# An encoder layer's last attention pair: the merge of three attention results spread over one unit more

## The reference, cut to what matters

```python
for w, d in ((128, 1), (512, 4), (2048, 16)):      # B heads: dilated windows
    o, lse = banded_attention(strided(q), strided(k), strided(v), ...)
w = jax.nn.softmax(jnp.stack(lses, 0), axis=0)
ob = jnp.einsum('cblh,cblhd->blhd', w, jnp.stack(outs, 0))
oa = rms_norm(oa, norm_a); ob = rms_norm(ob, norm_b)   # oa: windowed heads with a sink logit
x = layer_norm(ALPHA * x + concat([oa, ob]) @ w_out)
x = layer_norm(ALPHA * x + moe(x))                     # 16 experts, top 2, and a shared one
```

## Time and profile before

| | |
|---|---|
| median of 3 runs | 1217.55 us (1215.06 to 1222.8) |
| the profiled execution | 1218.93 us, of which 1217.1 us lie between its first and last instruction |
| PE busy | 1198.4 us (98% of the span) |
| DVE, ACT, POOL busy | 724.5, 591.5, 218.2 us |
| mean granted TensorE clock | 0.997 |
| granted TensorE clock from 590 to 620 us | 1.00 |
| PE's waits from 588 to 660 us | 2.9 us for exponentials (0.56, 0.72, 0.51, 0.49, 0.19 and 0.46), 1.2 us for the first low part of the transposes, 0.7 us for POOL's casts, 0.6 us for a residual, 0.5 us for the last results |

### The profile page before, as it was taken

The page is one execution under the profiler, slowest core; times in us unless marked ns, Lnnn a source line. Parts: engine busy times, 40 slices in busy tenths (PEclk is TensorE's granted clock), DMA queues, the critical chain, the costliest instruction groups (busy, mean ns, idle before and its releaser), DMA issues.

```text
span 1217.1 us, 22117 instructions
## 1 busy us (share of the span) xinstructions
PE 1198.4 (98%) x8040; PEld 1076.1 (88%) x8040; DVE 724.5 (60%) x1796; ACT 591.5 (49%) x1463; POOL 218.2 (18%) x276
## 2 busy tenths in 40 slices
PE   9999999999999999999999999999999999999998
PEld 9998888888888888888777888899989999999896
DVE  3222455655565556555877778568856566656358
ACT  4332344544454445444552434254557666756566
POOL 1121001200120012001211211000224323423223
PEclk9999999999999999999999999999999999999999
DMA  9787674365436643667854333592999999999995
GB/s 277 225 300 226 156 195 101 79 162 139 101 80 152 149 101 79 157 162 215 264 172 186 124 122 131 187 360 94 321 303 247 291 277 270 286 290 268 353 313 200
DMA packets 164676, 246.93 MB, mean 203 GB/s; under 512 B 41536, under 2 KB 111424, under 8 KB 163776
## 3 DMA queue, kind: packets, MB, share of 16 engines
q1 hardware_dynamic: 149408, 190.72, 51.4%
q0 software_dynamic: 11776, 41.95, 14.0%
q10 hardware_dynamic: 3408, 13.16, 2.7%
HBM read 150.59 MB, written 65.31 MB: 177 GB/s over the span
## 4 chain that ended last, share of the span: by engine, by line
PE 74%; issue 12%; DMA 4%; DVE 3%; POOL 3%; SPq 2%; ACT 1%; POOLq 1%; ACTq 0%; DVEq 0%
PE bank L916 16%; PE bank L918 16%; PE bank L917 16%; PE bank L1049 9%; PE bank L1036 5%; PE bank L1027 4%; PE bank L910 3%; PE bank L1028 3%; DMA raw_gu<-in_w_up 2%; POOL c_work L2509 1%; DVE c_work L2056 1%; DVE c_work L2054 1%; DVE w_gu_lo L2163 1%; SPq L615 1%; POOL Q L2536 1%
## 5 line engine op out<-in xcount | busy, mean ns | idle before, releaser
L1516 ACT ACTIVATE b_work<-b_work 128x256 f32<-128x256 f32 (+3 forms) x288 | 148.1, 514 | 230.0 <-DVE b_work L1969 230.0
L916 PE MATMUL bank<-xgT_hi,w_gu_hi 128*128 128x224 f32 (+1 forms) x704 | 195.6, 278 | 1.2 <-DVE c_work L2038 0.9
L918 PE MATMUL bank<-xgT_hi,w_gu_lo 128*128 128x224 f32 (+1 forms) x704 | 194.7, 277 | 0.0
L917 PE MATMUL bank<-xgT_lo,w_gu_hi 128*128 128x224 f32 (+1 forms) x704 | 194.7, 277 | 0.0
L1978 DVE COPY b_work<-bank 128x256 f32<-128x256 f32 (+2 forms) x256 | 112.8, 441 | 114.8 <-PE bank L1036 113.9
L916 PEld LDWEIGHTS bank<-xgT_hi,w_gu_hi 128*128 128x128 f32 x704 | 135.0, 192 | 3.0 <-issue 1.5
L917 PEld LDWEIGHTS bank<-xgT_lo,w_gu_hi 128*128 128x128 f32 x704 | 135.0, 192 | 0.8
L918 PEld LDWEIGHTS bank<-xgT_hi,w_gu_lo 128*128 128x128 f32 x704 | 135.0, 192 | 0.0
L2536 POOL CAST Q<-Q 128x512 fp32r<-128x512 f32 x48 | 53.3, 1141 | 432.1 <-DVE w_k_lo L1908 226.2
L1036 PE MATMUL bank<-keep,b_work 128*128 128x128 f32 x608 | 114.2, 274 | 3.2 <-ACT b_work L1516 3.2
L1036 PEld LDWEIGHTS bank<-keep,b_work 128*128 128x128 f32 x608 | 79.1, 139 | 36.3 <-ACT b_work L1516 8.0
(11 more groups left out here) (244 smaller groups left out, 2831.0 us busy)
## 6 DMA issues: line engine op xcount, KB each, us to landing
raw_gu<-in_w_gate SPq DMA_DIRECT2D x32, 512.0 KB, 8.7
raw_gu<-in_w_up SPq DMA_DIRECT2D x32, 512.0 KB, 9.6
raw_d<-in_w_down SPq DMA_DIRECT2D x16, 1024.0 KB, 9.7
Q<-stage_hi SPq DMA_DIRECT2D x96, 128.0 KB, 2.4
Q<-stage_lo SPq DMA_DIRECT2D x96, 128.0 KB, 2.4
o_scratch<-b_work SPq DMA_DIRECT2D x36, 264.0 KB, 3.4
wo_scratch<-a_work POOLq DMA_DIRECT2D x16, 512.0 KB, 4.4
w_o<-wo_scratch SPq DMA_DIRECT2D x16, 512.0 KB, 5.8
```

Of the source, the lines that this page charges most:

```text
L916: nc.tensor.matmul(o, w_hi, x_hi, start=first, stop=False)
L917: nc.tensor.matmul(o, w_hi, x_lo, start=False, stop=False)
L918: return nc.tensor.matmul(o, w_lo, x_hi, start=False, stop=last)
L1516: nc.scalar.activation(prob[:, u % 2, 0:n], prob[:, u % 2, 0:n], ACT.Exp, scale=-1.0, bias=o[:, HD:HD + 1], accum_out=o[:, HD + 1:HD + 2])\
```

## The change

The tables move everything from the squares on one unit later. The factors are cut in two: the three sums (`merge_sums`) stay in unit m+3, the reciprocals and weights (`merge_factors(t, s, False)`) go into unit m+4, and the four long operations go from m+4..m+7 to m+5..m+8. MERGES stays, so the maxima stay. Tile 0 has six output products inside the units (66 to 71) and ten behind them, where there were seven and nine. Outside the last pair `merge_factors` does what it did.

```diff
-SQUARES = (57, 63)
-SCALED = (60, 66)
-OT_UNIT, OT1_UNIT = 62, 70
-OP_UNIT = 65
-OP_UNITS = 7
+SQUARES = (58, 64)
+SCALED = (61, 67)
+OT_UNIT, OT1_UNIT = 63, 71
+OP_UNIT = 66
+OP_UNITS = 6
...
                         if g == m + 3:
-                            merge_factors(t, t % 2)
-                        if m + 4 <= g <= m + 7:
-                            merge_rows(t, t % 2, (g - m - 4,))
+                            merge_sums(t, t % 2)
+                        if g == m + 4:
+                            merge_factors(t, t % 2, False)
+                        if m + 5 <= g <= m + 8:
+                            merge_rows(t, t % 2, (g - m - 5,))
...
-            def merge_factors(t, s):
+            def merge_sums(t, s):
                 dve.wait_ge(S["merge_exp"], t + 1)
                 V.tensor_tensor(mL, mD[:, 0:3, :], heads(s)[:, :, :, HD + 1], ALU.mult)
                 dve.drain()
                 V.tensor_tensor(mR[:, 0, :], mL[:, 0, :], mD[:, 3, :], ALU.add)
                 V.tensor_tensor(mR[:, 1, :], mL[:, 1, :], mL[:, 2, :], ALU.add)
+
+            def merge_factors(t, s, sums=True):
+                if sums:
+                    merge_sums(t, s)
                 dve.drain()
                 V.reciprocal(mR, mR)
```

## The result

The changed kernel takes 1223.18 us in the median of 18 runs (1221.8 to 1227.19), the kernel before 1217.6 (1214.2 to 1224.03, 18 runs). The ratio is 1.0046, 95% interval 1.0034 to 1.0057: 5.6 us slower, 4.1 to 6.9. The forecast was 2.7 us slower, 1220.3, with a range of 1215.5 to 1224.0. The profiled execution took 1225.87 us, 1224.0 of them between first and last instruction.

The account below looks back on a forecast made before the run. PE, busy 1198.4 of 1217.1 us, was taken as the bound. A loss of 2.0 us up to the first output product plus 0.7 at the pair's end, 2.7, on the median 1217.55 gave 1220.3 us, range 1215.5 to 1224.0.

Parts of the forecast that it names:

- the most likely case: Whole kernel: the loss as forecast, 2.7 us, without a fall of the clock, giving 1220.3 us; chance 50%.
- The rival of the falling clock: PE's idling halves its clock if the qk(64) wait nears 3 us; 1221.5 to 1223.7 us; chance 20%.
- the chain: From qk(64) through bias, exponential, scaling, transposes and DVE's copy to the first output product at 618.1: 2.0 us lost.
- The first half of the change: Factors in two units on DVE: gain of 0.4 us up to unit 61, between 0 and 1.2, paid back next.
- The casts: POOL's last four casts wait for later squares: start 606.7, qk(64) at 609.2, PE waits some 2.1 us.
- Tile 0's transposes and the first product: Behind qk(65), PE waits 1.2 us for the second scaling; first output product at 618.1, 2.0 us lost.
- The end of the pair: Behind the last unit, PE waits 1.15 us for the last results instead of 0.47: 0.7 us more.
- it gains: Rival: second scaling or POOL not late, only waits for exponentials shrink; 1217.0 us, or 1216.3; chance 12%.
- no difference: Rival: waits just move, the chain behind qk(64) loses what DVE wins; 1217.5 to 1218.5 us; chance 18%.

Follow-up runs that it names:

- twelve fillers: Changed kernel plus twelve matmuls nobody reads on PE, eight ahead of unit 64's scores, four ahead of tile 0's transposes; ratio 1.0009 to the kernel before.
- the split alone: Kernel before with only the factors split, first long operation in the same unit as the weights, all tables as before; ratio 0.9997.
- all repairs: Changed kernel, no added matmuls: roots between casts, both tile 0 scalings in unit 61, tile 2's maxima in 62, tile 1's transposes in 70; ratio 0.9982.
- POOL delayed: Kernel before with one more pair of inverse roots, results unused, on POOL ahead of the last four casts; ratio 1.0020.
- shift alone: Changed kernel without the split: all six factor operations in unit m+3, tables as changed; ratio 1.0065 to the kernel before.
- eight fillers: Changed kernel plus eight matmuls nobody reads on PE ahead of unit 64's scores only; ratio 1.0032 to the kernel before.

## Why the prediction was right, and where it was wrong

The measured 1223.18 us lies in the forecast range, near its upper end. That is in part luck: the most likely case, 1220.3, didn't happen. The rival of the falling clock had 1221.5 to 1223.7, but made up of up to two falls of 1.7 us, where one long fall cost 3.7; and its own condition, a wait near 3 us at unit 64, wasn't met (1.99).

- **Direction, range and the chain:** right. The forecast case, full clock, is the trace with twelve fillers: 2.0 us at the first product and 2.6 at tile 2's transposes, forecast 2.0 and 2.7. What the changed kernel itself lost, 5.6 us, is twice that.
- **The first half of the change** as a gain of 0.4, given back: the split alone is worth nothing (0.9997). That it seems to be worth some 2 us inside the shift I didn't see; the sum had it only as the 0.83 us that the square comes earlier.
- **The casts:** 606.43 against 606.7, unit 64 at 609.07 against 609.2, the wait 1.99 against 2.1. The first two casts took 2.6 us, inside 2.18 to 3.05.
- **Tile 0's transposes and the first product:** the wait of 1.07 for the scaling (1.2) was worth 0.7 us at the product, and the maxima behind the long operation 0.6, each in one trace. The forecast 1.3 us wait at the first product read 0.43 in the changed kernel, since PE was then too slow to arrive early, and 1.16 with fillers.
- **The end of the pair:** 0.6 us (0.7).
- **The clock** is the step that failed: the fall was left out of the sum, and as a rival ("The clock falls") it had a chance of a fifth and "up to 1.7 us more" for one fall, taken from the fall near 894 us in the trace of before, in a stretch where PE had all its work ready. What happened is this rival, with 13.7 us at half clock and 3.7 us lost (of 6.8 us of full-speed time; part of the rest is waits that PE has anyway at full clock, 0.98 and 1.16 us with the twelve fillers). Two things were off. I compared the longest single wait (2.1) with the one that had brought a fall (2.99), while in the runs falls also came with waits of 1.93 and 1.99 us, behind three of about 1 us in a row, and even with a single one of 0.90. And I took the length of the half clock from a single case, of 3.4 us. That case was also read a little wrong: the fall began at 893.5, 1.0 us after PE resumed and not 0.7.
- **The rivals "it gains" and "no difference"** fall: the ratio's interval begins at 1.0034.
- The base is no part of the error: the median of 18 runs of before is 1217.6, where 1217.55 was used.

Left open: why the half clock lasts 13.7 us in the changed kernel and 3.4 in others, what makes it come in one execution and not in the next of the same kernel, and some 1 to 2 us with all repairs. The changed kernel's trace also has a fall of 3.4 us at 798.5 that the trace of before hasn't. Ten of the fourteen traces have it there (between 791 and 806), always with the same wait of 0.9 us; the kernel before with POOL delayed and the one with all repairs are among them, so it is no mark of the change.

## What to carry to other kernels

When a change makes the busiest engine wait, price the wait twice: once as idle time, and once as what the clock may do with it. Don't take a wait for harmless because a longer one is known to have brought a fall: here the longest wait didn't decide, and no other rule was found that fits all traces. A wait moved the odds and the length of a half clock, and it takes many runs, with the mean clock of each, to see that. Moving a step by one unit moves it behind whatever the other queues hold in that unit: the three losses here (squares ahead of the casts, a scaling behind an exponential, maxima behind a long operation) were all visible in the order of the queues. Each wait could be undone by itself, though undoing the first brought a new one behind it. Fillers in a wait are a cheap test of whether the clock takes part: if added work makes a kernel faster, and its granted clock stays up, it does.

## What the runs showed of the hardware

- The granted clock fell to half (the lower of its two levels, 1.2 GHz) in or behind one wait of 1.93 to 2.59 us (POOL delayed, changed kernel, shift alone), behind one of 1.27 us, and with eight fillers behind waits of 1.07, 0.98 and 1.17 us. In other single traces waits of 1.16 us and of 1.27, 0.97 and 1.16 us from 590 to 620 us brought none.
- With one wait of 0.90 to 0.94 us near 791 to 801 us the clock fell in ten traces and with one of 0.91 or 0.95 it didn't in four. Near 890 to 900 us it fell with waits of 2.35, 2.37, 2.71 and 2.99 us, and not with 0.41 and 1.62.
- Between the marks it came back after 3.4 us in four traces, after 13.7 us in three (the changed kernel among them) and after 17.1 us with the shift alone. PE was busy in nearly all of the longer times (the stretch from 623 to 624: 1.00 busy, clock 0.50).
- The kernel before has half clocks too. Of its 98 runs beside the experiments, the ten with a mean clock of 1.000 took 1216.4 us on average, the sixteen with 0.995 or less 1222.1.
- Twelve more matmuls of 0.23 us made the changed kernel 4.5 us faster by the two ratios. The Trainium skill (TensorE: Matmul & The Clock Gate, Why this matters for your kernels) warns of gaps between matmul bursts. These runs agree that gaps matter. But the gaps it warns of are longer than any between the marks, and there the clock fell with waits of 2.59 us and less, down to one of 1.27.
- Casts on POOL took 1.1 us beside light DVE work and 1.3 beside its long products (2.61 for two). Beside the casts such a product took 1.01 and 1.39 us in the changed kernel, instead of 0.68.
